# A router with its norm and shift moved behind the products, and a top-64 selection in two halves

## The reference, cut to what matters

```
h    = rms_norm(x, norm2_g) * (1 + sc2) + sh2
aff  = softmax(h @ w_router)                      # 512 x 16
gate, idx = top_k(swapaxes(aff, 1, 2), 64)        # for each expert its 64 best tokens
xe   = h[idx]
hid  = silu(xe @ w_gate) * (xe @ w_up)            # 64 x 1024 for each expert
ye   = (hid @ w_down) * gate
x    = x + g2 * zeros.at[idx].add(ye)
```

## Time and profile before

| what | value |
| --- | --- |
| median of 3 runs | 1971.48 us (1966.75 to 1973.75) |
| profiled execution, own time | 1966.23 us |
| profiled execution, span | 1964.9 us |
| mean granted clock of TensorE in it | 0.953 |
| busy PE / PEld / DVE / ACT / POOL | 89% / 58% / 41% / 29% / 6% |
| bytes moved by DMA | 329.39 MB |

### The profile page before, as it was taken

One profiled execution on the slowest core, in us unless ns is written; L12 is line 12 of the kernel. 1 busy time (PEld: TensorE's weight loads), 2 busy tenths in 40 slices (PEclk: granted clock), 3 DMA queues, 4 the chain that ended last, 5 costly groups with the idle time before them and its releaser, 6 DMA issues.

```text
span 1964.9 us, 20245 instructions
## 1 busy us (share of the span) xinstructions
PE 1758.2 (89%) x8127; PEld 1137.8 (58%) x8127; DVE 803.8 (41%) x1313; ACT 560.5 (29%) x983; POOL 123.1 (6%) x127
## 2 busy tenths in 40 slices
PE   5999899887999885998888888999888899999998
PEld 2656567556778652333333333687544578888786
DVE  2154755566433433111111112538566534444443
ACT  2224553554423331000000000431544442222221
POOL 0002021113000001000000000000100100011100
PEclk9999799987999886999999999999889899999999
DMA  8221201123512336999999999243400122223301
GB/s 302 94 65 43 86 22 65 44 89 126 151 57 95 150 150 263 423 423 425 424 423 424 424 424 416 83 152 86 129 1 1 44 86 86 86 86 106 109 1 44
DMA packets 92257, 329.39 MB, mean 168 GB/s; under 512 B 7428, under 2 KB 22404, under 8 KB 67588
## 3 DMA queue, kind: packets, MB, share of 16 engines
q1 hardware_dynamic: 85408, 315.80, 41.5%
q10 hardware_dynamic: 5412, 8.03, 1.2%
q0 software_dynamic: 1344, 4.25, 0.6%
HBM read 322.82 MB, written 4.19 MB: 166 GB/s over the span
## 4 chain that ended last, share of the span: by engine, by line
PE 71%; DMA 10%; DVE 10%; ACT 5%; issue 3%; ACTq 0%; SPq 0%; DVEq 0%
PE PS L658 21%; PE PS L776 11%; PE PS L1007 9%; PE PS L401 7%; DMA ring<-in_w_exp_gate_dram 4%; DMA room<-in_w_exp_gate_dram 4%; PE PS L397 3%; PE PS L532 3%; PE PS L787 3%; PE PS L614 2%; PE PS L842 2%; PE PS L457 1%; PE PS L679 1%; DMA ring<-in_w_in_dram 1%; PE PS L957 1%
## 5 line engine op out<-in xcount | busy, mean ns | idle before, releaser
L1717 DVE TENSOR_TENSOR wR<-ring,wR 128x1024 fp32r<-128x1024 f32 (+2 forms) x134 | 151.4, 1130 | 234.6 <-ACT wR L1120 234.5
L1120 ACT CAST wR<-ring 128x1024 fp32r<-128x1024 f32 (+2 forms) x134 | 130.0, 971 | 210.4 <-PE PS L1007 128.2
L1007 PE MATMUL PS<-wR,hR 128*128 128x512 f32 x768 | 177.8, 393 | 8.9 <-DVE tmp L2434 6.9
L658 PE MATMUL PS<-xR,wR 128*128 128x512 f32 x768 | 175.6, 390 | 0.0
L1007 PEld LDWEIGHTS PS<-wR,hR 128*128 128x128 f32 x768 | 144.7, 189 | 42.0 <-DVE tmp L2434 9.6
L658 PEld LDWEIGHTS PS<-xR,wR 128*128 128x128 f32 x768 | 144.0, 188 | 30.3 <-issue 0.4
L658 PE MATMUL PS<-hR,wR 128*128 128x512 f32 x528 | 132.0, 409 | 7.9 <-DVE hR L2415 3.3
L776 PE MATMUL PS<-room,xeT 128*64 128x512 f32 x512 | 115.0, 602 | 14.6 <-DMA room<-in_w_exp_gate_dram 14.6
L776 PE MATMUL PS<-ring,xeT 128*64 128x512 f32 x512 | 116.1, 607 | 13.1 <-DMA ring<-in_w_exp_gate_dram 12.4
L658 PEld LDWEIGHTS PS<-hR,wR 128*128 128x128 f32 x528 | 102.0, 195 | 36.2 <-issue 9.4
L658 PE MATMUL PS<-hR1h,wR 128*128 128x512 f32 x320 | 107.7, 409 | 8.3 <-DVE hR1m L2094 7.4
(11 more groups left out here) (423 smaller groups left out, 2665.5 us busy)
## 6 DMA issues: line engine op xcount, KB each, us to landing
ring<-in_w_exp_gate_dram SPq DMA_DIRECT2D x32, 1024.0 KB, 26.9
room<-in_w_exp_up_dram SPq DMA_DIRECT2D x32, 1024.0 KB, 26.5
ring<-in_w_exp_down_dram SPq DMA_DIRECT2D x32, 1024.0 KB, 26.7
room<-in_w_exp_gate_dram SPq DMA_DIRECT2D x32, 1024.0 KB, 27.4
ring<-in_w_exp_up_dram SPq DMA_DIRECT2D x32, 1024.0 KB, 26.9
room<-in_w_exp_down_dram SPq DMA_DIRECT2D x32, 1024.0 KB, 27.1
ring<-in_w_mod_dram SPq DMA_DIRECT2D x12, 2048.0 KB, 8.0
ring<-in_w_in_dram SPq DMA_DIRECT2D x11, 2048.0 KB, 8.7
```

The lines of the kernel that those rows point to most:

```text
L658: mm = T.matmul(b, o[s][:, k, :], x(t, k), start=(k == ks[0] and j == 0), stop=(k == ks[-1] and j == 2))
L1007: mm = T.matmul(down[m], uR[:, r % 2, s, k, 128 * i:128 * i + 128], o[t][:, 0, 512 * q:512 * q + 512], start=(k + j == 0), stop=(k == 3 an ...
L1120: A.copy(parts(wR, chunks, n)[0], W.view(unit)[:, ks, cs]).then_inc(act_hi.sem, act_hi.up(key))
L1717: V.tensor_tensor(lo, W.view(unit)[:, ks, cs], hi.bitcast(F32), ALU.subtract) \
```

## The change

1. The router's weights are multiplied by the norm's gain in `mix` (`router_weights`, new, on DVE), and the shift's part of the logits becomes a row `crow`, added later. The logits are made from `xT` itself, and the root of the mean square is applied to them by token (`rinvc`, four values per partition, by Sqrt and a reciprocal). `h2T` is gone.
2. The sums of squares and the logits are made in two halves of four tiles (`half`, new), each as four 32-column products side by side; the sums behind each tile are gone.
3. The rows for the scratch memory are transposed from `xT`; ACT multiplies them by the inverse root by token as it takes them. Three of the eight are transposed before the affinities, five after.
4. The selection works on 64 partitions (32 for each half, 16 of them in use) by 256 tokens, eight rounds in both halves at once. The halves are merged: the best 64 of one in falling order against the best 64 of the other in rising order, and by place the larger is taken.
5. Scale and shift by column are applied to the gathered rows, on ACT, in eight passes of 128 columns for each pair in place of two copies of 512. They come from `fold` over a small scratch write and read (`foldd`), both on ACT's queue.
6. The rooms are released earlier and their order is changed: the first pair's gate units take four ring slots and the four places in rooms 2 and 3, released by "xk" (the last transpose of `xk`) and "uT" (the last split of `uT`); its up units take four ring slots and the four places of "mixed", released by the second half of the sums.
7. The gate product starts when the first half of the gathered rows is there.

```diff
             if k == 2:
-                slots = [(at + turn) % NS if turn < NS else turn]
+                cycle = [(at + j) % NS for j in range(NS)]
+                cycle[4:4] = range(NS + 4, NS + 8)
+                slots = [(cycle + list(range(NS, NS + 4)))[turn]]
...
-             [(what, room[:, i, :]) for what, room in zip(("mixed", "mixed", "h2k", "h2T"), rooms) for i in range(2)])
+             [(what, room[:, i, :]) for what, room in zip(("mixed", "mixed", "xk", "uT"), rooms) for i in range(2)])
...
+        def half(total, raw, n):
+            T.wait_ge(*dve_mix["wr"])
+            T.wait_ge(*dve_mix["y", 4 * n + 3])
+            for k in range(4 * n, 4 * n + 4):
+                r = 32 * (k % 4)
+                mm = T.matmul(raw[r:r + 32, :], wr[:, k, :], xT[:, k, :], start=(n == 0), stop=(n == 1))
+            mm.then_inc(pe_mix.sem, pe_mix.up(("logits", n)))
+            T.wait_ge(*act_mix["sqy", 4 * n + 3])
+            for k in range(4 * n, 4 * n + 4):
+                r = 32 * (k % 4)
+                mm = T.matmul(total[r:r + 32, :], ones[:, 0:32], sqs[k % 4], start=(n == 0), stop=(n == 1))
+            mm.then_inc(pe_mix.sem, pe_mix.up(("sums", n)))
...
+                    if br and t == 3:
+                        b = pool.take(T, "fold", dve_mix["foldT"])
+                        T.wait_ge(*dve_mix["wsum"])
+                        T.matmul(b[:, 0:16], ones, wsum, start=True, stop=True)
+                        turn(b[0:16, 128:256], fold).then_inc(pe_mix.sem, pe_mix.up("fold"))
...
-                    if t:
-                        T.wait_ge(*act_mix["sqy", t - 1])
-                        squares([total], [ones], t - 1, 8, pe_mix, ("sqy", t - 1))
-            T.wait_ge(*act_mix["sqy", 7])
-            squares([total], [ones], 7, 8, pe_mix, ("sqy", 7))
+                    if t == 4:
+                        half(total, raw, 0)
+            turn_rows(six, 0, 0)
+            half(total, raw, 1)
...
-            for k in range(8):
-                r = 32 * (k % 4)
-                T.wait_ge(*act_moe["h2T", k])
-                mm = T.matmul(b[r:r + 32, :], wr[:, k, :], h2T[:, k, :], start=(k < 4), stop=(k >= 4))
+            turn_rows(pool, 1, 0)
             for i in range(4):
                 mm = turn(b[:, 128 * i:128 * i + 128], mrow[:, 128 * i:128 * i + 128])
+            for i in range(4):
+                mm = T.matmul(b[:, 8 * i:8 * i + 8], rinv[:, 128 * i:128 * i + 128], ones[:, 0:8], start=True, stop=True)
+            mm.then_inc(pe_moe.sem, pe_moe.up("square"))
+            turn_rows(pool, 2, 0)
-            for i in range(4):
-                mm = turn(b[0:16, 128 * i:128 * i + 128], lgt[:, i, :])
+            for u in range(2):
+                mm = turn(b[0:64, 128 * u:128 * u + 128], lgt2[:, u, :])
+            for i, q in ((0, 1), (1, 1), (2, 1), (3, 0), (3, 1)):
+                turn_rows(pool, i, q)
-            for n, src in enumerate((gv, ifl)):
+            for n, (src, h) in enumerate(((gv, 0), (ifl, 0), (gr, 1), (ifl, 1))):
...
+                    if name == "gate" and kq % 2 == 0:
+                        T.wait_ge(*act_moe["xe", p, kq // 2])
...
-            inverse_root(rinv, bank("total1")[:, 0:512], 1.0 / 1024, s, "rinv")
+                    if t == 1:
+                        A.wait_ge(s_fold, 16)
+                        A.dma_start(fine, foldd.rearrange("x (p k) -> p x k", k=8)).then_inc(s_fold, 16)
...
-                A.activation(h2T[:, k, :], h2T[:, k, :], ACT.Identity, bias=modc[:, 24 + k, 0:1]) \
+            A.activation(rinvc, bank("square")[:, 0:32].rearrange("p (i x) -> p i x", x=8)[:, :, 0], ACT.Sqrt, bias=eps,
+                         scale=1.0 / (32 * 1024)).then_inc(s.sem, s.up("rms"))
-                    A.copy(by_eight(h2k[:, i, :], q), bank(("h2k", i, q)).rearrange("t (p k) -> t k p", k=8)) \
+                A.activation(by_eight(h2k[:, i, :], q), bank(("h2k", i, q)).rearrange("t (p k) -> t k p", k=8), ACT.Copy,
+                             scale=rinvc[:, i:i + 1]).then_inc(s.sem, s.up(("h2k", i, q)))
+            A.copy(gr, gv[:, ::-1]).then_inc(s.sem, s.up("gr"))
...
-                    A.copy(xeT[:, 4 * q:4 * q + 4, p % 2, :], bank(("xe", p, q)).rearrange("p (k s) -> p k s", k=4)) \
+                    for k in range(4 * q, 4 * q + 4):
+                        c = A.activation(xeT[:, k, p % 2, :], bank(("xe", p, q))[:, 128 * (k % 4):128 * (k % 4) + 128],
+                                         ACT.Identity, bias=fine[:, 1, k:k + 1], scale=fine[:, 0, k:k + 1])
...
-                V.scalar_tensor_tensor(h2T[:, k, :], xT[:, k, :], AB[:, 0, k:k + 1], rinv, ALU.mult, ALU.mult) \
+            V.tensor_copy(rinv, bank("total1")[:, 0:512]).then_inc(s.sem, s.up("sums"))
+            V.reciprocal(rinvc, rinvc).then_inc(s.sem, s.up("rinvc"))
+            V.tensor_tensor(lgt, lgt, rinvc.unsqueeze(2).broadcast_to([128, 4, 16]), ALU.mult).then_inc(s.sem, s.up())
+            V.tensor_tensor(lgt, lgt, crow.unsqueeze(1).broadcast_to([128, 4, 16]), ALU.add).then_inc(s.sem, s.up())
-            V.tensor_copy(aff, bank("aff")[0:16, 0:512]).then_inc(s.sem, s.up("aff"))
+            V.tensor_copy(aff, bank("aff")[0:64, 0:256]).then_inc(s.sem, s.up("aff"))
-            V.tensor_copy(ifl, iu).then_inc(s.sem, s.up("topk"))
+            V.tensor_copy(ifl[0:32, :], iu[0:32, :]).then_inc(s.sem, s.up())
+            V.tensor_copy(ifl[32:64, :], iu[32:64, ::-1]).then_inc(s.sem, s.up("topk"))
-            V.tensor_copy(idx, bank("gi")[:, 8:16]).then_inc(s.sem, s.up("idx"))
+            V.tensor_copy(both, bank("gi")[:, 0:32].rearrange("p (a b) -> p a b", a=4)).then_inc(s.sem, s.up("gi"))
+            V.tensor_tensor(more, both[:, 0], both[:, 2], ALU.is_ge).then_inc(s.sem, s.up())
+            V.scalar_tensor_tensor(off, both[:, 3], 256.0, both[:, 1], ALU.add, ALU.subtract).then_inc(s.sem, s.up())
+            V.tensor_tensor(off, off, more, ALU.mult).then_inc(s.sem, s.up())
+            V.scalar_tensor_tensor(idx, both[:, 3], 256.0, off, ALU.add, ALU.subtract).then_inc(s.sem, s.up("idx"))
...
-        W.free["mixed"] = pe_mm[("wo", 7), 0]
+        W.free["xk"], W.free["uT"], W.free["mixed"] = pe_mix["xT", 7], dve_mix["uR", 7], pe_mix["sums", 1]
         router()
-        W.free["h2T"], W.free["h2k"] = pe_moe["h2k", 3, 1], (s_h2, 16)
```

More of the change, by code:

```diff
@@ L393, in pe @@
     def pe(T):
-        every = Banks(0, 8)
+        every, six = Banks(0, 8), Banks(0, 6)
         def turn(dst, src, k=128):
@@ L683, in gate_tiles, with turn_rows @@
                         yield
+        def half(total, raw, n):
[10 more added lines that the diff above has]
+            mm.then_inc(pe_mix.sem, pe_mix.up(("sums", n)))
+        def turn_rows(pool, i, q):
+            b = pool.take(T, ("h2k", i, q), act_moe["h2k", i, q])
+            for k in range(4):
+                mm = turn(b[:, 128 * k:128 * k + 128], xT[:, 4 * q + k, 128 * i:128 * i + 128])
+            mm.then_inc(pe_moe.sem, pe_moe.up(("h2k", i, q)))
         def mix():
@@ L716, in mix @@
                             T.wait_ge(*dve_mix["uR", k])
-                        total = Banks(6, 7).take(T, "total1", act_mix["rinv"])
+                        total = Banks(6, 7).take(T, "total1", dve_moe["sums"])
+                        raw = Banks(7, 8).take(T, "logit", dve_moe["logit"])
                     chunk_tile(pool, key, w, mix_chunks, n, hR1, range(8), dve_mix["y", t])
-                    if t:
-                        T.wait_ge(*act_mix["sqy", t - 1])
-                        squares([total], [ones], t - 1, 8, pe_mix, ("sqy", t - 1))
-            T.wait_ge(*act_mix["sqy", 7])
-            squares([total], [ones], 7, 8, pe_mix, ("sqy", 7))
-        def router():
-            b = every.take(T, "logit", dve_moe["logit"])
-            T.wait_ge(s_wr, 16)
-            for k in range(8):
-                r = 32 * (k % 4)
-                T.wait_ge(*act_moe["h2T", k])
-                mm = T.matmul(b[r:r + 32, :], wr[:, k, :], h2T[:, k, :], start=(k < 4), stop=(k >= 4))
-            mm.then_inc(pe_moe.sem, pe_moe.up("logit"))
-            b = every.take(T, "logitT", dve_moe["logitT"])
+                    if t == 4:
+                        half(total, raw, 0)
+            turn_rows(six, 0, 0)
+            half(total, raw, 1)
+        def router():
+            pool = six
+            turn_rows(pool, 1, 0)
+            b = pool.take(T, "logitT", dve_moe["logitT"])
             T.wait_ge(*dve_moe["logit"])
@@ L1368, in after @@
                             A.copy(xT[:, k, :], bank(("xT", k))).then_inc(s.sem, s.up(("xT", k)))
+                    if br and t == 5:
+                        A.wait_ge(*dve_mix["foldT"])
+                        A.dma_start(foldd.rearrange("x (k p) -> (x k) p", p=128), foldT).then_inc(s_fold, 16)
                     if br == 0 and t == 7:
@@ L2065, in head, with router_weights @@
                     .then_inc(s.sem, s.up(("on", h)))
+            def router_weights():
+                shift = modc[:, 24:32, 0]
```

(28 more changed lines are left out.)

74 lines of the change are left out of this document (41 added, 33 removed).

## The result

The changed kernel took 1952.70 us (median of 4 runs, 1945.55 to 1956.13) beside 1969.92 us (1966.75 to 1973.75) for the kernel before: a ratio of 0.9907 over all runs, 95% interval 0.9887 to 0.9927, or 18.3 us less (the medians by themselves differ by 17.2). Run again beside eleven runs of the kernel before, it took 1950.45 (1948.99 to 1951.75) for 1969.67, a ratio of 0.9897 (0.9880 to 0.9914), or 20.3 us less, with an interval of 16.9 to 23.6 (medians: 19.2). The forecast was 20.5 us less, at 1951.0. The first profiled execution took 1954.31 us, its span is 1953.0 and its mean granted clock 0.955.

A forecast was written before the change was run, and what follows sets the result against it. The expert weight stream was taken as the bound, so an earlier first gate quarter ends the kernel equally earlier. Projection 3.2, chain to MAX8 9.7, selection 6.1, merge -1.6, gather 3.1: 20.5 us off 1971.48, 1951.0 us; range 1944 to 1961.

The forecast's parts named there:

- table loads in the path: Rival, chance 0.05: the Sqrt table load waits for the narrow products and costs 1.3 us; gain 19, 1952.5 us.
- about 6 a pair: Expert stage: PE's slack against the weight stream for each pair of experts, in us, from 37.4 us over the stage.
- Projection, 3.2: Output projection: squares summed once for the half instead of behind each tile, 34.8 us against 38.0, 3.2 gained.
- To the first MAX8, 8.6: Last projection tile to first MAX8: the new chain takes 8.6 us where the old took 18.3.
- the Sqrt table loads while PE sums: Chain to the first MAX8: Sqrt's table load is hidden beside PE's sums; only 0.25 us counted for Sqrt.
- Selection, 6.1: Selection: 23 passes over 256 columns, not 512, save 0.265 us each, 6.1 in all; bounds nothing and 7.8.
- the largest rival: Chance 0.17: selection hardly shrinks, or the short chain has twice the handovers; gain 12.5 us, 1959.
- Merge, 1.6 lost: Joining the halves before the gather: 2.75 us where 1.16 stood, a loss of 1.6; bounds 1.0 and 3.
- Gather, 3.1 gained: First gather of rows: 4.3 us for 7.39, as no weight units run beside it; bounds 0 and 3.1.
- The rows in scratch: Write of rows before the first gather: lands at 735 or 736.5, index at 737.5, so hidden by 1 us.
- Scale and shift, level: Gathered rows on ACT: level at the first gate product; later pairs delay the down product 1.8 us, inside the slack.
- Rooms, nothing by itself: Buffer places for weight units: order changes, count stays 16 units, so no gain by itself.

## Why the prediction was right, and where its steps were not

The total was right: 20.5 us forecast, 20.3 measured again and 18.3 at first. An agreement to 0.2 is closer than the runs can tell (16.9 to 23.6), and in part luck, since steps that were off by up to 1.4 us cancel below. The total alone doesn't separate the forecast from its rival *table loads in the path* (gain 19) either; the trace does, and that rival's condition held. The main mechanism was right: whatever the first down load gained, the end gained. That was tested from both sides. The router was varied from 34.4 to 44.7 us, and the experts took 451.2 to 451.7 in all of these; only the 32-column passes moved them. No run put the norm's passes back ahead of the logits, so the 8.3 us gained up to the first MAX8 rest on the two chains and not on an experiment. The slack that the forecast took as "about 6 a pair" is 37.4 / 8 = 4.7; nothing hung on it, as 1.2 us a pair were added. Point by point, by the forecast's own steps:

- **Projection, 3.2:** 3.1. The half costs 0.99 + 0.86 = 1.85 for the 1.92 of the earlier trace rows.
- **To the first MAX8, 8.6:** 9.94, so 1.3 too short. The step that failed is "the Sqrt table loads while PE sums". The load began at 728.36, right behind the narrow products for which Sqrt waited, as in the rival *table loads in the path*, which gave it a chance of 0.05 and a price of 1.3. Moving it ahead won 1.5 at this point. The Trainium skill (ScalarE: Activation LUTs, What ACT_TABLE_LOAD costs) adds a drain of 1.38 us to each switch. By that rule two switches would have cost 2.8 us more; the chain shows 0.01 us between the end of each load and its function (729.64 to 729.65, 731.22 to 731.23), so here the load's own 1.28 us is all. The Exp table's load ran beside DVE's five passes, as forecast.
- **Selection, 6.1:** 0.26 off each pass, as taken: 23 passes lasted 744.87 - 733.45 = 11.4 us for 17.4. The bound at nothing, on which the largest rival rested, is out; taking the halves out lost 4.8 with the merge counted in.
- **Merge, 1.6 lost:** 747.58 - 744.87 = 2.7 for the 1.5 us from 753.80 to 755.29 of before, a loss of 1.2. The five small passes took 0.09 to 0.20, where I had 0.21 with gap.
- **Gather, 3.1 gained:** 4.30 for 7.39, as taken; with units beside it, 8.50. The estimate of 3.2 that stood beside it in the forecast was 1.1 too short.
- **The rows in scratch:** the forecast had 1 us of margin, the trace 2.4. It is the steepest edge of this design: with eight units ahead of it the write takes 17.67 us.
- **Scale and shift, level:** the eight passes last 2.90 us, as computed, and delay each down product by 1.2 us ((15.2 - 5.8) / 8) for the 1.8 forecast. With 64-column passes, 2.9 us a pair more than before the change, the slack still covers it; with 32 it does not. In the first pair "level" was nearly right: from the first transposition to the gate product it is 2.92 us for 2.65 of before (762.73 to 765.38), and two copies there, started by halves as the passes are, would be 0.9 shorter still. What lies after the landing became 0.4 shorter all the same, since the first quarter took 5.75 for 6.45; that is the granted clock (0.63 for 0.57), which no term of the forecast held.
- **Rooms, nothing by itself:** here the reason was wrong. I counted the units and not when SP could issue them. The order decides how many are sent just before the write, and with the old one the gather waits for the write and starts 8.3 us later. The gain of the gather and the safety of the write both hang on it.

The two sizes that were off (1.4 too much gained to MAX8, 0.4 too much lost in the merge) and the 0.4 and 0.3 gained after the landing, which the forecast did not have, make up the difference between 20.5 and 20.0, but for 0.1 each in the projection and the selection.

Of the signs that the forecast named, two did not come: the first MAX8 was 9.94 and not within 9 us of the last tile, and the first gather, counted from the start of the projection, came 16.2 us earlier and not 18. The others did: MAX8 at 0.42, the gather at 4.3, a period of 60.6, and, with the 8.5 us taken off by which the projection started later in this execution, the first down load at 752.1 (for 751) and the end of the last down product at 1203.4 (for 1203).

## What to carry to other kernels

Where a saturated weight stream bounds a stage, shorten the chain up to the first release of its buffers and cost nothing inside the stage until the slack is used up; here 9 and 23 us more waiting for ACT than in the kernel before were free and 50 were not. Before you value an order of buffers at nothing, ask which loads it sends out ahead of the small transfers in the serial chain: eight loads of 1 MB more than doubled the time of a 2 MB write. An activation whose table is not loaded and whose input comes late can have a dummy of the same function ahead of its wait: here that won 1.5 us up to the first MAX8, though no gain of the whole kernel could be told from the scatter.

## What the runs showed of the hardware that was not expected

- In this kernel an ACT table load was not taken ahead of the waits of the instruction that needs it: ACT idled, and the load began only when the input was there (728.36, behind PE's 727.35 + 0.92).
- With the old order of places the write on ACT's queue, issued behind a batch of loads on SP's, came through no sooner than about all of them together: the 2 MB write landed at 752.06, and the ten megabytes from 723.41 on would take until about 748 at the 424 GB/s of the page's expert slices.
- With PE idle for the selection (window 740 to 745 us, below), the granted clock is 0.50, which is the lower of its two levels, 1.2 of 2.4 GHz, and it is back at 1.00 only in 760 to 765. The first gate quarter therefore takes 5.75 us for 3.65. Idle products in the gap bring it to 3.69 but run at the low clock themselves.

```profile
740.00:745.00 5.00, 0.00 (x0) 0.00 (x0) 4.66 (x17) 0.24 (x1) 0.00 (x0) 0.50 0.93 329
760.00:765.00 5.00, 5.00 (x26) 1.82 (x24) 0.00 (x0) 0.00 (x0) 0.00 (x0) 1.00 0.67 238
```

- When PE waited for ACT longer once a pair, the granted clock fell as well: 0.91 in 900 to 1100 us with 32-column passes, against 0.99 in the changed kernel. PE's products then took 5.6 us longer over the stage (411.23 for 405.65), so of the 20 us some 14.3 are the waits and 5.6 the slower products.
